# Two value groups moved behind the keys, and the second attention run from query tile 3 down to tile 0

## What is computed

```python
q_a = (rms_norm_2(c_q, q_norm_g) @ w_uq).reshape(B, S, A_HEADS, QK_NOPE + QK_ROPE)
q_nope = q_a[..., :QK_NOPE]
q_rope = apply_rope(q_a[..., QK_NOPE:], cos[:, None, :], sin[:, None, :])
kv = (rms_norm_2(c_kv, kv_norm_g) @ w_ukv).reshape(B, S, A_HEADS, QK_NOPE + V_HEAD)
k_nope, v_a = kv[..., :QK_NOPE], kv[..., QK_NOPE:]
k_rope = apply_rope(k_r, cos, sin)
y_a = chunk_causal_mla_attention(q_nope, q_rope, k_nope, k_rope, v_a)
...
s = (einsum('bqhd,bkhd->bhqk', qn, k_nope) + einsum('bqhr,bkr->bhqk', qr, k_rope)) * scale
s = where(key_chunk[None, :] <= q_chunk[:, None], s, -inf)
p = softmax(s, axis=-1)
return einsum('bhqk,bkhd->bqhd', p, v)
...
merged = g_m * (y_m @ w_branch_m) + g_a * (y_a @ w_branch_a)
```

## Time and profile before

| | |
|---|---|
| median of 3 runs | 1713.38 us |
| the three runs | 1708.16, 1713.38, 1725.19 us |
| the profiled execution | 1726.52 us |
| its span | 1724.5 us |
| its mean granted TensorE clock | 0.94 of full |
| TensorE busy | 1549.4 us, 90% |
| VectorE, ScalarE, GpSimd busy | 795.1, 456.5, 591.3 us |

### The profile page before, as it was taken

How to read it: one execution, slowest core, us unless ns; L and a number is a source line. 1 busy time by engine, 2 the same in 40 slices (tenths; PEclk the granted TensorE clock), 3 DMA queues, 4 the chain that set the end, 5 groups by cost and what they waited for, 6 DMA issues and landing times.

```text
span 1724.5 us, 24166 instructions
## 1 busy us (share of the span) xinstructions
PE 1549.4 (90%) x9824; PEld 1292.6 (75%) x9824; DVE 795.1 (46%) x1476; ACT 456.5 (26%) x716; POOL 591.3 (34%) x477
## 2 busy tenths in 40 slices
PE   6879999889999999979999999999999959987782
PEld 5867887878989898967999878775578956544441
DVE  2344757358787874247314620434512344432334
ACT  4233334233132313233323332332223220000001
POOL 2472121234454454423533144520044303322222
PEclk9988999899999999989999999986999979989996
DMA  5231010125445442213222122310033568999994
GB/s 220 74 123 49 25 50 25 68 80 195 182 160 196 181 182 77 103 50 122 105 74 74 50 73 98 106 50 1 1 147 147 223 246 300 380 395 378 401 386 161
DMA packets 36926, 256.89 MB, mean 149 GB/s; under 512 B 7232, under 2 KB 7872, under 8 KB 13008
## 3 DMA queue, kind: packets, MB, share of 16 engines
q1 hardware_dynamic: 31056, 246.94, 37.7%
q0 software_dynamic: 5760, 8.41, 1.5%
HBM read 250.59 MB, written 15.20 MB: 154 GB/s over the span
## 4 chain that ended last, share of the span: by engine, by line
PE 80%; DVE 8%; issue 5%; ACT 3%; POOL 2%; DMA 1%; SPq 0%; DVEq 0%; POOLq 0%; ACTq 0%
PE G L1936 18%; PE G L1938 18%; PE G L1937 18%; PE SA L2437 4%; PE G L2437 4%; POOL wl L683 2%; PE SA L2331 2%; PE G L1958 2%; PE OB L2100 2%; PE PB L2445 1%; PE SA L2330 1%; PE OB L2347 1%; PE OB L2259 1%; PE PB L2090 1%; PE PB L2338 1%
## 5 line engine op out<-in xcount | busy, mean ns | idle before, releaser
L683 POOL TENSOR_TENSOR wl<-raw,wh 128x512 fp32r<-128x512 f32 x364 | 490.9, 1381 | 754.8 <-ACT wh L810 745.1
L810 ACT ACTIVATE wh<-raw 128x2048 fp32r<-128x2048 f32 x91 | 173.9, 1911 | 259.5 <-PE G L1938 255.0
L1936 PE MATMUL G<-Hh,wh 128*128 128x512 f32 x544 | 216.3, 398 | 5.8 <-DVE arena L1404 1.7
L1936 PE MATMUL G<-wh,Yh 128*128 128x256 f32 (+2 forms) x700 | 206.4, 295 | 15.4 <-POOL wl L683 10.4
L1938 PE MATMUL G<-Hh,wl 128*128 128x512 f32 x544 | 212.9, 391 | 0.0
L1937 PE MATMUL G<-Hl,wh 128*128 128x512 f32 x544 | 212.8, 391 | 0.0
L1937 PE MATMUL G<-wl,Yh 128*128 128x256 f32 (+2 forms) x700 | 204.5, 292 | 0.0
L1938 PE MATMUL G<-wh,Yl 128*128 128x256 f32 (+2 forms) x700 | 204.5, 292 | 0.0
L1936 PE MATMUL G<-wh,Hh 128*128 128x256 f32 x640 | 186.4, 291 | 1.0 <-DVE arena L1215 1.0
L1938 PE MATMUL G<-wh,Hl 128*128 128x256 f32 x640 | 181.7, 284 | 0.0
L1937 PE MATMUL G<-wl,Hh 128*128 128x256 f32 x640 | 181.7, 284 | 0.0
(11 more groups left out here) (440 smaller groups left out, 2407.0 us busy)
## 6 DMA issues: line engine op xcount, KB each, us to landing
raw<-in_pieces_dram SPq DMA_DIRECT2D x91, 1024.0 KB, 4.9
arena<-in_pieces_dram SPq DMA_DIRECT2D x24, 1024.0 KB, 4.7
arena<-in_wexp_dram SPq DMA_DIRECT2D x11, 2048.0 KB
dn_w<-in_wexp_dram SPq DMA_DIRECT2D x22, 1024.0 KB, 33.9
arena<-in_wexp_dram SPq DMA_DIRECT2D x12, 1024.0 KB
gu_y<-in_wexp_dram SPq DMA_DIRECT2D x6, 2048.0 KB, 38.4
gu_h<-in_wexp_dram SPq DMA_DIRECT2D x6, 2048.0 KB
gu_l<-in_wexp_dram SPq DMA_DIRECT2D x6, 2048.0 KB
```

The costliest lines, as they stand in the source:

```text
L683: ins = pool.tensor_tensor(low_[:, part], whole[:, part], high[:, part], ALU.subtract)
L810: act.activation(wh[:, split_slot(s)], wait_raw(act, sp_list[s]), ACT.Copy).then_inc(S("high_split"), 1)
L1936: pe.matmul(out, ah, bh, start=first, stop=False)
```

## The change

The value groups are spread: groups 0 to 3 go one behind each rope group, 4 and 5 follow, then the turnings of the rotated rows and the key groups, and value groups 6 and 7 go behind the keys. ScalarE copies them in this order, and makes the high part of the key weights after value group 2 and that of the first gate piece in step 8 of the attention (since its slot is held by the value weights until value group 7). The sum of values of the first unit waits until value group 7 is freed. The units run in the order of query tiles 3, 2, 1, 0, and the turned outputs go to the places of the tile concerned.

```diff
--- before.py
+++ after.py
@@ -177,10 +177,11 @@
     g += [("qn", h, "a") for h in range(AH)]
     g += [("krT", 0, "v")]
     for t in range(NT):
-        g += [("qr", t, "v")]
-    g += [("va", i, "a") for i in range(8)]
+        g += [("qr", t, "v"), ("va", t, "a")]
+    g += [("va", i, "a") for i in (4, 5)]
     g += [("qrT", t, "v") for t in range(NT)]
     g += [("kn", h, "a") for h in range(AH)]
+    g += [("va", i, "a") for i in (6, 7)]
     g += [("yaT", i, "v") for i in range(8)]
     for j in range(4):
         g += [("ga", 2 * j + f, "a") for f in range(2)]
@@ -524,7 +525,8 @@
 
         units = [(ty, q, h) for ty in range(2) for q in range(NT) for h in range(NH)]
         munits = [(h, q) for h in range(MH) for q in range(NT)]
-        aunits = [(q, h) for q in range(NT) for h in range(AH)]
+        AQ = (3, 2, 1, 0)
+        aunits = [(q, h) for q in AQ for h in range(AH)]
         M0, A0 = len(units), len(units) + len(munits)
         MSCALE = 0.25 * 128 ** -0.5
         ASCALE = 192 ** -0.5
@@ -1052,16 +1054,22 @@
                     free_group(act.activation(qn[:, h, :], b[:, :], ACT.Copy), "qn", h)
             high(s)
             s += 1
+
+            def value_rows(i):
+                b = wait_group(act, "va", i)
+                free_group(act.activation(va[:, i // 2, (i % 2) * 512:(i % 2 + 1) * 512], b[:, :], ACT.Copy), "va", i)
+
+            for i in range(3):
+                value_rows(i)
             high(s)
             s += 1
-            for i in range(8):
-                b = wait_group(act, "va", i)
-                free_group(act.activation(va[:, i // 2, (i % 2) * 512:(i % 2 + 1) * 512], b[:, :], ACT.Copy), "va", i)
-            high(s)
-            s += 1
+            for i in range(3, 6):
+                value_rows(i)
             for h in range(AH):
                 b = wait_group(act, "kn", h)
                 free_group(act.activation(kn[:, h, :], b[:, :], ACT.Copy), "kn", h)
+            for i in range(6, 8):
+                value_rows(i)
 
             def aunit(u):
                 q, h = aunits[u]
@@ -1071,12 +1079,16 @@
                                accum_out=rsum2[:, (q % 2) * 8 + h:(q % 2) * 8 + h + 1]).then_inc(S("probs_ready"), 1)
 
             for t in range(len(aunits) + 4):
+                if t == 8:
+                    high(s)
+                    s += 1
                 if t < len(aunits):
                     aunit(t)
                 if t >= 11 and (t - 11) % 8 == 0:
-                    q = (t - 11) // 8
+                    o = (t - 11) // 8
+                    q = AQ[o]
                     for i in range(2):
-                        b = wait_group(act, "yaT", 2 * q + i)
+                        b = wait_group(act, "yaT", 2 * o + i)
                         act.activation(Yhv[:, 4 * i:4 * i + 4, q * P:(q + 1) * P], b[:, :].rearrange("p (f n) -> p f n", f=4), ACT.Copy).then_inc(S("yaT_high"), 1)
             for j in range(4):
                 high(s)
@@ -1689,8 +1701,8 @@
                 j = (q % 2) * 8 + h
                 dve.wait_ge(S("values_summed"), A0 + u + 1)
                 own(dve.reciprocal(rinv[:, j:j + 1], rsum2[:, j:j + 1]))
-                if h == 0 and q:
-                    wait_group(dve, "yaT", 2 * q - 1)
+                if h == 0 and u:
+                    wait_group(dve, "yaT", 2 * (u // AH) - 1)
                 dve.tensor_scalar(ya[:, h * P:(h + 1) * P], OB[:, 0:P], rinv[:, j:j + 1], None, ALU.mult).then_inc(S("a_out"), 1)
 
             for t in range(len(aunits) + 4):
@@ -1701,12 +1713,13 @@
                 if 0 <= t - 1 < len(aunits):
                     acopied(t - 1)
                 if t >= 11 and (t - 11) % 8 == 0:
-                    q = (t - 11) // 8
+                    o = (t - 11) // 8
+                    q = AQ[o]
                     for i in range(2):
-                        b = wait_group(dve, "yaT", 2 * q + i)
-                        dve.wait_ge(S("yaT_high"), 2 * q + i + 1)
+                        b = wait_group(dve, "yaT", 2 * o + i)
+                        dve.wait_ge(S("yaT_high"), 2 * o + i + 1)
                         free_group(dve.tensor_tensor(Ylv[:, 4 * i:4 * i + 4, q * P:(q + 1) * P], b[:, :].rearrange("p (f n) -> p f n", f=4),
-                                                     Yhv[:, 4 * i:4 * i + 4, q * P:(q + 1) * P].bitcast(F32), ALU.subtract), "yaT", 2 * q + i)
+                                                     Yhv[:, 4 * i:4 * i + 4, q * P:(q + 1) * P].bitcast(F32), ALU.subtract), "yaT", 2 * o + i)
             def merged_low(f):
                 dve.wait_ge(S("merged_high"), f + 1)
                 dve.tensor_tensor(Hlv[:, f, :], merged[:, f, :], Hhv[:, f, :].bitcast(F32), ALU.subtract).then_inc(S("merged_low"), 1)
@@ -2300,24 +2313,36 @@
                 features("qn", ("qn", j), 4 * j, ng=4, act=(Ch, Cl), kts=range(3), ncols=512)
             pe.wait_ge(S("kr_turned"), 1)
             transposes("krT", 0, [kr2[:, t].rearrange("p u n -> p (u n)") for t in range(NT)])
-            a, b = (w[:, 0:1536].rearrange("p (k n) -> p k n", n=512) for w in weights(("qr",)))
-            for t in range(NT):
+            def rope_rows(t, w):
                 bank = group("qr", t)
                 for k in range(3):
-                    ins = split3(bank[:, :], (Ch[:, k, t * P:(t + 1) * P], Cl[:, k, t * P:(t + 1) * P]), (a[:, k, :], b[:, k, :]), k == 0, k == 2)
+                    ins = split3(bank[:, :], (Ch[:, k, t * P:(t + 1) * P], Cl[:, k, t * P:(t + 1) * P]), (w[0][:, k, :], w[1][:, k, :]), k == 0, k == 2)
                 filled(ins)
-            a, b = (w.rearrange("p (k n) -> p k n", n=1024) for w in weights(("va",)))
-            for i in range(8):
+
+            def value_rows(i, w):
                 t, half = divmod(i, 2)
+                cols_ = slice(half * 512, (half + 1) * 512)
                 bank = group("va", i)
                 for k in range(2):
                     ins = split3(bank[:, :], (Ch[:, 3 + k, t * P:(t + 1) * P], Cl[:, 3 + k, t * P:(t + 1) * P]),
-                                 (a[:, k, half * 512:(half + 1) * 512], b[:, k, half * 512:(half + 1) * 512]), k == 0, k == 1)
+                                 (w[0][:, k, cols_], w[1][:, k, cols_]), k == 0, k == 1)
                 filled(ins)
+
+            wr = [w[:, 0:1536].rearrange("p (k n) -> p k n", n=512) for w in weights(("qr",))]
+            rope_rows(0, wr)
+            wv = [w.rearrange("p (k n) -> p k n", n=1024) for w in weights(("va",))]
+            value_rows(0, wv)
+            for t in range(1, NT):
+                rope_rows(t, wr)
+                value_rows(t, wv)
+            for i in (4, 5):
+                value_rows(i, wv)
             for t in range(NT):
                 wait_freed(pe, "qr", t)
                 transposes("qrT", t, [qrr[:, t, c * P:(c + 1) * P] for c in range(4)])
             features("kn", ("kn",), 0, ng=8, act=(Ch, Cl), kts=range(3, 5), ncols=1024)
+            for i in (6, 7):
+                value_rows(i, wv)
             wait_freed(pe, "kn", 7)
             wait_freed(pe, "qrT", 3)
             wait_freed(pe, "krT", 0)
@@ -2341,6 +2366,8 @@
             def avalues(u):
                 q, h = aunits[u]
                 pe.wait_ge(S("pt_copied"), A0 + u + 1)
+                if u == 0:
+                    wait_freed(pe, "va", 7)
                 if u:
                     pe.wait_ge(S("a_out"), u)
                 for k in range(q + 1):
```

## The result

| | before | after |
|---|---|---|
| median | 1711.03 us | 1720.47 us |
| lowest and highest | 1708.07 and 1725.32 us | 1716.51 and 1724.23 us |
| runs | 20 (17 at 1708 to 1713.4, 3 at 1723 to 1725.3) | 20 |
| profiled execution (span) | 1726.52 us (1724.5) | 1724.23 us (1722.2) |

The ratio is 1.0043, with an interval of 1.0026 to 1.0060. It lies near the ratio of the means (1.0042), in which the three upper runs of before count; the ratio of the medians is 1.0055. The same holds for the ratios of the experiments. The change makes the kernel slower, by 9.4 us between the medians. By the two profiled executions it would be 2.3 us faster, and that contradiction is the subject of this study.

What follows compares the result with a forecast made beforehand. TensorE, busy 90% of the span and partly at half clock, was taken as the bound. Front +4.4, order -17.7 and late loss +5 made -8.3 us, off the 1713.38 median: 1705 us, range 1696 to 1723.

Steps and rivals of the forecast that it cites:

- The sum: Whole kernel: 4.4 - 17.7 + 5 = -8.3 us; 1718.2 from the profiled execution, 1705 off the timed median.
- Rival 3: Attention's start: in most timed runs of before the clock doesn't fall, so +9.4 us is left, 1723; chance 0.15.
- Front, +4.4: Projections: 2.4 us with the 5.8 us wait for value weights, plus 2.0 for half clock behind it.
- rival 1: Attention's end: the clock is not lost in tile 0, so -13.3 us, 1700; chance 0.15.
- Order, -17.7: Attention: tiles 3, 2, 1, 0 at full clock throughout take 87.9 us in place of 105.56.
- late loss, +5: Attention's last units (tile 0) and first gate pieces: half clock costs +5 us, between 0 and 9.
- Rival 2: Attention: the clock falls in tile 1 already, at the turning among its units; +1.4 us, 1715; chance 0.2.
- Moved high part and its GpSimd instructions, 0: Attention: the first gate piece's high part behind unit 7, and its low part on GpSimd, cost 0 us.

Runs made afterwards that it cites:

- experiment 1: Also called before_again: the kernel before, no edit, executed again for a second trace; 1706.01 us, attention 85.89 us.
- experiment 4: The kernel after, with value groups 0 to 2 multiplied by the rope weights already there; 1726.64 us (ratio 1.0078), projections 34.19 us.
- experiment 9: Against before: two value groups behind the keys, others in turns from the third rope group on, tile 0 first; 1706.10 us, ratio 0.9958.
- experiment 3: The kernel before with only the order of tiles changed to 3, 2, 1, 0; 1716.43 us, ratio 1.0017.
- experiment 7: The kernel before with only the order of tiles changed, to 3, 2, 0, 1; 1720.14 us, ratio 1.0034.
- experiment 8: The kernel before with only the order of tiles changed, to 2, 1, 0, 3; 1714.95 us, ratio 0.9989.
- the second execution: The kernel after, no edit, executed again for a second trace; 1721.68 us, attention 91.41 us.
- experiment 2: The kernel after with the old order of tiles 0, 1, 2, 3, so the projections' change alone; 1714.44 us, ratio 1.0006 against before.
- experiment 6: Against before: two value groups behind the keys, six in a row behind the rope groups, tile 0 first; 1708.41 us, ratio 0.9972.
- experiment 10: Against before: two value groups behind the keys, others in turns from the second rope group on, tile 0 first; 1709.19 us, ratio 0.9964.
- the repeat: The kernel of experiment 6, unchanged, run again against before; 1708.58 us, ratio 0.9968.

## Why the prediction was wrong

**The step that failed** is in "The sum": "It lies above all three timed runs (1708.16 to 1725.19); I take the difference off their median of 1713.38: 1705." The difference of -8.3 us held a term of -17.7 that exists only in an execution whose clock falls at 1148. The median run is most likely not such a one (experiment 1). The profile had warned twice: the profiled execution lay above every timed run, and two of these three lay 12 and 17 us below the highest, about the size of that term. Rival 3 describes what happened, with its mechanism and point of decision, at 1723 us against 1720.5 measured. It got 0.15 because the one trace was given more weight than the two lower times; by the 94 runs its condition held in some three of four.

The terms themselves, against the trace they were made from:

- *Front, +4.4.* Measured +4.55 (41.73 against 37.18). The idle time is 5.33 us in place of 5.8, value group 5 waits 0.93 in place of 0.6, and the key weights come in time where 1.1 was set. The half clock lasts 5.4 us behind the gap, so it costs some 2.7 in place of 2.0 (an estimate, half of its length). With no gap in experiment 4, and with one of 1.54 us in experiment 9, there is none. But the forecast set it against a front that stays at full clock, and three of five traces of that front don't. Its rival 1 leaned on the same stretch (1.83 us busy in 5.15, no fall at 1118.90); in before_again and in experiments 3, 7 and 8 the clock falls there.
- *Order, -17.7, and late loss, +5.* In the attention they made -14.15 (105.56 to 91.41), and behind it +1.3, in the second execution +2.9: -12.8 to -11.3 against -12.7. The clock held through tiles 3, 2 and 1, a unit of tile 1 took 1.88 us where 1.87 was said, and the clock fell behind the turning in tile 0, as argued. Rival 2, a fall in tile 1, occurred in no trace. A unit of tile 0 at full clock takes 1.19 us, not 1.4 (experiment 1).
- *Moved high part and its GpSimd instructions, 0.* Confirmed by the starts of the units of tile 2 beside them, the same as in experiment 3.
- *The sum.* From 1726.52 the forecast gave 1718.2; the two profiled executions of after took 1724.23 and 1721.68. Of the 6 us to the first, 1.6 lie between the turned latents and the key rope's turning (23.26 us against 21.65, through a half clock of 3.4 us near 1095 that other kernels of this study have or lack without regard to their edits), 2.3 in the experts' stage (265.04 against 262.78 between the first and last gate-and-up matmul), and 2.3 ahead of the turned latents, where nothing was edited.

**What stands in place of the forecast:** against an execution of before at full clock, +4.4 in the projections, +5.5 in the attention and +1.3 to +2.9 in the first gate pieces, 11.2 to 12.8 by the traces, and 9.4 by the medians. But the trace of before_again lies 5 us under the median beside it. It lacks the half clock between 1090 and 1099, which 11 of the 14 traces have (1.6 us), and its front, at 37.30, lies 2.1 under what the same code took in experiment 3. Against that front the change costs 2.3 us there, and 9.1 to 10.7 in all, which fits the medians better. Which front most timed runs of before have is not shown.

**Why the start of the attention matters.** In before the first scores stand 0.69 us behind the last key group; with value groups last they start at once. Of 54 runs of kernels with two value groups last and tile 0 first (experiments 2, 6, 9, 10, with the repeat) none was above 1717.3, while 21 of 94 runs of before were at 1722.9 or above. So the part "two behind the keys" seems to take the slow start away, which is a gain of its own: the mean of a set of runs has it, the median hardly. The idle moment alone doesn't do it: it stands ahead of tile 3 or 2 in experiments 3, 7 and 8 too, and their three traces hold the clock there. This is argued from the counts and not shown: no run took the 0.69 us away by itself, and why the same stretch of work leads to a fall in one execution and not in the next stays open. The Trainium skill (TensorE: Matmul & The Clock Gate, Part 1) says that how many matmuls run at the low clock at a kernel's start differs from run to run, and that this cost is under 1% of a typical span. No run here shows that at the start, where the trace of before has the full clock (1.00 in the windows 14.50 to 20.00 and 20.00 to 60.00). The step of some 15 us in 1711, 0.9%, lies in the midst of the kernel; it is of that size, and still larger than the whole change.

## What to carry to other kernels

When the profiled execution lies above every timed run, look in its clock row for a long half-clock stretch before costing anything against it, and make the sum for an execution without it too: a change that "removes" such an episode gives the median nothing. A group that is moved ahead as cover is worth it only from the place where its own weights are ready; two rope groups too early here made 41.73 us of what could be 35.33. And of the orders tried here, the short units did best at the start without an idle moment ahead (an attention of 85.9 us), next with the longest ones behind them (89.5), then last (90.3 and 91.4), and worst with units of tile 1 behind them (97.6).

## What the runs showed of the hardware

- The same program, with the same 3.33 us of work in 4.20 us ahead, went on at 2.4 GHz in one execution and at 1.2 GHz for 47.8 us in another. While it was at the low level TensorE was 98% busy (29.38 us with 28.77 busy in tile 1), and that didn't lift it at once.
- How long it stayed low went with the work behind the fall: 6.8 us with tile 3 behind (one trace), 17 to 20.5 with the end of tile 0 and the gate pieces (five), 27.3 with tile 1 (one), 47.8 with tiles 0 and 1 (one). Two half clocks that began near the first gate piece, in experiment 8 and in the second of 9 and 10, lasted 3.4 us.
- The front of before, the same code each time, held 2.4 GHz in one trace (37.18 us), lost it for 3.4 us in another (37.30) and for 6.8 in three (39.44 to 39.47).
- Units of tile 0 and tile 1 at the attention's start held 2.4 GHz once they had it, with TensorE 98% and 89% busy (10.93 in 11.12, 14.99 in 16.80).
